# Borders of a two-layer streaming encoder: first rows and weights loaded one stage ahead, input normalisation on three engines

## The reference

```python
x = layernorm(x)                                   # once, ahead of the first layer
for l in range(2):
    h = x @ w_in[l]                                # 1024 -> 7592 columns: q, k, v of three mixers, gates
    oa, ob, oc = forgetting attention, banded attention with sinks, latent attention
    up_n = (o_n * silu(g_n)) @ w_br[l, n]          # n = a, b, c: 512 -> 1024
    mixed = sum_n sigmoid(gate_n) * up_n
    x = layernorm(alpha * x + mixed @ w_o[l])
```

## Time and profile before

| | |
|---|---|
| time, median of 3 runs | 3544.3 us (3537.41, 3544.3, 3546.9) |
| the profiled execution | 3536.73 us, span 3535.1 us |
| TensorE matmul busy | 3212.8 us (91%), 20878 instructions |
| VectorE busy | 1463.6 us (41%) |
| ScalarE busy | 882.9 us (25%) |
| GpSimd busy | 173.4 us (5%) |
| DMA | 421.83 MB, mean 119 GB/s |

### The profile page before, as it was taken

The page is one execution under the profiler, slowest core; times in us unless marked ns, Lnnn a source line. Parts: engine busy times, 40 slices in busy tenths (PEclk is TensorE's granted clock), DMA queues, the critical chain, the costliest instruction groups (busy, mean ns, idle before and its releaser), DMA issues. The chain is left out here.

```text
span 3535.1 us, 52710 instructions
## 1 busy us (share of the span) xinstructions
PE 3212.8 (91%) x20878; PEld 2646.8 (75%) x20878; DVE 1463.6 (41%) x3367; ACT 882.9 (25%) x1990; POOL 173.4 (5%) x118
## 2 busy tenths in 40 slices
PE   0999998999999996989969999989999999977988
PEld 0888897777887774667758888877778887755867
DVE  6214234444454442354631142444445444324556
ACT  1221223333223332220212212223332233322110
POOL 0000000101111100000000000001011111000000
PEclk9999999999999997999979999999999999988999
DMA  5332316423332317664443322362222422096633
GB/s 186 125 106 89 91 48 199 115 69 83 87 104 81 87 34 188 203 237 143 142 143 108 105 92 73 103 198 75 70 78 84 118 80 64 28 279 211 203 128 113
DMA packets 405226, 421.83 MB, mean 119 GB/s; under 512 B 146432, under 2 KB 314240, under 8 KB 402624
## 3 DMA queue, kind: packets, MB, share of 16 engines
q1 hardware_dynamic: 375824, 380.74, 35.0%
q10 hardware_dynamic: 29168, 37.89, 3.3%
HBM read 293.27 MB, written 127.64 MB: 119 GB/s over the span
## 5 line engine op out<-in xcount | busy, mean ns | idle before, releaser
L376 PE MATMUL proj_acc<-proj_wh,keep_xh 128*128 128x512 f32 (+1 forms) x1296 | 503.5, 388 | 12.4 <-DVE proj_wl L340 12.4
L377 PE MATMUL proj_acc<-proj_wl,keep_xh 128*128 128x512 f32 (+1 forms) x1296 | 501.9, 387 | 0.0
L378 PE MATMUL proj_acc<-proj_wh,keep_xl 128*128 128x512 f32 (+1 forms) x1296 | 501.5, 387 | 0.0
L1222 ACT ACTIVATE att_p<-att_ss,att_stat 128x257 f32<-128x257 f32 (+9 forms) x384 | 249.2, 649 | 641.1 <-DVE att_stat L1272 602.3
L1279 DVE COPY att_pt<-att_tr 128x256 f32<-128x256 f32 (+3 forms) x384 | 177.1, 461 | 550.2 <-PE att_tr L1159 549.9
L1272 DVE TENSOR_REDUCE att_stat<-att_ss 128x1 f32<-128x257 f32 (+9 forms) x384 | 245.6, 640 | 117.0 <-PE att_ss L1150 112.5
L1148 PE MATMUL att_ss<-att_kt,att_qt 96*128 96x512 f32 (+7 forms) x768 | 291.2, 487 | 1.4 <-DVE att_kt L1207 1.4
L376 PEld LDWEIGHTS proj_acc<-proj_wh,keep_xh 128*128 128x128 f32 x1296 | 245.3, 189 | 58.7 <-DVE proj_wl L340 13.2
L378 PEld LDWEIGHTS proj_acc<-proj_wh,keep_xl 128*128 128x128 f32 x1296 | 245.0, 189 | 46.2
L377 PEld LDWEIGHTS proj_acc<-proj_wl,keep_xh 128*128 128x128 f32 x1296 | 245.2, 189 | 45.4
L1159 PE MATMUL att_tr<-keep_ident,att_p 128*128 128x128 f32 x1392 | 236.0, 283 | 30.6 <-DVE att_sgt L1295 15.7
(11 more groups left out here) (328 smaller groups left out, 5489.7 us busy)
## 6 DMA issues: line engine op xcount, KB each, us to landing
up_gates<-scratch_gates SPq DMA_DIRECT2D x18, 1536.0 KB, 8.0
scratch_gates<-att_gout SPq DMA_DIRECT2D x208, 128.0 KB, 1.7
proj_raw<-in_w_in SPq DMA_DIRECT2D x48, 512.0 KB, 3.7
att_graw<-in_w_in SPq DMA_DIRECT2D x44, 512.0 KB, 3.9
str_ka<-in_cache_a_kT SPq DMA_DIRECT2D x16, 1024.0 KB, 8.9
str_va<-in_cache_a_v SPq DMA_DIRECT2D x16, 1024.0 KB, 5.4
scratch_sg<-proj_out SPq DMA_DIRECT2D x54, 256.0 KB, 2.1
att_sg<-scratch_sg SPq DMA_DIRECT2D x24, 512.0 KB, 5.7
```

Source lines behind the costliest of these rows:

```text
L376: nc.tensor.matmul(bank, hi, wh[:, u, kt, 0:w], start=kt == 0, stop=False)
L377: nc.tensor.matmul(bank, hi, wl[:, u, kt, 0:w], start=False, stop=False)
L378: mm = nc.tensor.matmul(bank, lo, wh[:, u, kt, 0:w], start=False, stop=kt == KT - 1)
L1222: nc.scalar.activation(p[:, s, place], ss[:, s, place], ACT.Exp, bias=stat[:, m % 4, 0:1], accum_out=stat[:, m % 4, 1:2]).then_inc(exp_rea ...
```

## The change

- Input normalisation is shared by three engines. VectorE does statistics, reciprocal, a new one-column product (minus mean times reciprocal) and the gain; ScalarE scales and shifts (`Identity` with scale and bias); GpSimd adds the bias row. The gain of tile t-1 stands in VectorE's list behind the statistics of tile t. A tile is stored two tiles later, and VectorE waits for gain and bias only behind the first statistics.
- `early2` is kept for the whole program (it also serves as `C["row"]`, which has the same size), and holds three of the four quarters of the next projection's first weights; `C["early"]` holds its first three row tiles. They are loaded at the end of the input normalisation for layer 0 and in the middle (t = 5) of the output stage for layer 1; the load at t = 5 is issued after the second layer too.
- The projection's first tile: two tiles are turned instead of three, tile 0's rows are split, then the weights, then the rows of tiles 1 and 2; TensorE waits for each weight split by itself, and turns tile 2 behind tile 0.
- Up stage: three weight tiles are split before the channels of tile 0; TensorE's first tile waits for each weight split by itself. Of the output stage's weights five tiles are loaded ahead instead of six, and in the sixth place the first mixed rows.
- Output stage: the first mixed rows are in SBUF; three weight tiles are loaded there instead of two.

```diff
+            load_first_weights(sp, C, T, 0, first_loaded)
+            for t in range(EARLIEST):
+                load_first_rows(sp, C, T, t, first_loaded)
+            sp.wait_ge(first_loaded, 16 * (1 + EARLIEST))
...
                 act.wait_ge(var_ready, t + 1)
                 nc.scalar.activation(mv[:, t % 2, 2:3], mv[:, t % 2, 1:2], ACT.Sqrt,
                                      bias=C["eps"][:, 0:1]).then_inc(std_ready, 1)
-                if t >= 1:
-                    store(t - 1)
+                act.wait_ge(scale_ready, t + 1)
+                nc.scalar.activation(x[:, t % N, :], x[:, t % N, :], ACT.Identity, scale=mv[:, t % 2, 3:4],
+                                     bias=mv[:, t % 2, 4:5]).then_inc(centred, 1)
+                if t >= 2:
+                    store(t - 2)
+            store(NT - 2)
...
-            dve.wait_ge(gb_loaded, 32)
+            def by_gain(t):
+                dve.wait_ge(centred, t + 1)
+                nc.vector.tensor_tensor(x[:, t % N, :], x[:, t % N, :], gb[:, 0, :], ALU.mult).then_inc(scaled, 1)
             for t in range(NT):
                 dve.wait_ge(x_loaded[t % N], 16 * (t // N + 1))
-                norm_rows(nc, dve, ch, x[:, t % N, :], gb, st, mv[:, t % 2, :], var_ready, std_ready, t, normed)
+                m = mv[:, t % 2, :]
+                ch.link(nc.vector.bn_stats(st[:, 0, :], x[:, t % N, 0:512]))
+                ch.link(nc.vector.bn_stats(st[:, 1, :], x[:, t % N, 512:1024]))
+                nc.vector.bn_aggr(m[:, 0:2], st[:].rearrange("p a b -> p (a b)")).then_inc(var_ready, 1)
+                if t == 0:
+                    dve.wait_ge(gb_loaded, 32)
+                else:
+                    by_gain(t - 1)
+                dve.wait_ge(std_ready, t + 1)
+                ch.link(nc.vector.reciprocal(m[:, 3:4], m[:, 2:3]))
+                nc.vector.scalar_tensor_tensor(out=m[:, 4:5], in0=m[:, 0:1], scalar=-1.0, in1=m[:, 3:4],
+                                               op0=ALU.mult, op1=ALU.mult).then_inc(scale_ready, 1)
+            by_gain(NT - 1)
+        @block.gpsimd
+        def _(pool):
+            pool.wait_ge(gb_loaded, 32)
+            for t in range(NT):
+                pool.wait_ge(scaled, t + 1)
+                nc.gpsimd.tensor_tensor(x[:, t % N, :], x[:, t % N, :], gb[:, 1, :], ALU.add).then_inc(normed, 1)
...
-    raw = ph.sb("raw", [P, 4, 2, 512])
+    raw_last = ph.sb("raw_last", [P, 2, 512])
+    raw = [C["early2"][:, q, :].rearrange("p (h n) -> p h n", h=2) for q in range(FIRST_Q)] + [raw_last]
...
-            for t in range(NT):
-                if t >= XA:
-                    sp.wait_ge(x_taken, 2 * (t - XA + 1))
+            for t in range(XA, NT):
+                sp.wait_ge(x_taken, 2 * (t - XA + 1))
...
-                pe.wait_ge(x_loaded[t % XA], 16 * (t // XA + 1))
+                if t >= XA:
+                    pe.wait_ge(x_loaded[t % XA], 16 * (t // XA))
...
+                    if by_weights:
+                        pe.wait_ge(w_ready[0], kt + 1)
...
-            for t in range(XA):
+            for t in range(2):
                 turn(t)
-            pe.wait_ge(w_ready[0], KT)
+            pe.wait_ge(xl_made, 2)
             for t in range(NT):
                 pe.wait_ge(xl_made, 2 * (t + 1))
-                tile(0, 0, 512, t)
+                tile(0, 0, 512, t, by_weights=t == 0)
+                if t == 0:
+                    turn(2)
                 if t + XA < NT:
...
-            for q in range(4):
+            for q in range(FIRST_Q, 4):
...
-            for t in range(XA):
-                x_high(t)
+            x_high(0)
             for kt in range(KT):
                 split_hi(act, 0, 0, kt)
+            for t in range(1, XA):
+                x_high(t)
...
-            for t in range(XA):
-                x_low(t)
+            x_low(0)
             for kt in range(KT):
                 split_lo(dve, 0, 0, kt)
+            for t in range(1, XA):
+                x_low(t)
...
-EARLIEST, EARLY = 3, 6
+EARLIEST, EARLY, EARLY_O = 3, 6, 5
...
+FIRST_Q = 3
...
+def load_first_rows(eng, C, T, t, loaded):
+    eng.dma_start(C["early"][:, t, :], T["y_prompt"][0][rows(t)]).then_inc(loaded, 16)
+def load_first_weights(eng, C, T, l, loaded):
+    src = T["w_in"].rearrange("l (kt p) n -> l p kt n", p=P)[l, :, 0:2 * FIRST_Q, ds(CHUNKS[0][1][0][0], 512)]
+    eng.dma_start(C["early2"][:].rearrange("p k (h n) -> p (k h) n", h=2), src).then_inc(loaded, 16)
...
-                    sp.dma_start(C["early2"][:], w_o_tiles(T, l)[:, EARLIEST:EARLY, :]).then_inc(early_loaded, 16)
-            sp.wait_ge(early_loaded, 32)
+                    sp.dma_start(C["early2"][:, 0:EARLY_O - EARLIEST, :], w_o_tiles(T, l)[:, EARLIEST:EARLY_O, :])\
+                        .then_inc(early_loaded, 16)
+                if t == 5:
+                    sp.wait_ge(stored[0], 16)
+                    sp.dma_start(C["early2"][:, EARLY_O - EARLIEST, :], S["mix"][rows(0)]).then_inc(early_loaded, 16)
+            sp.wait_ge(early_loaded, 48)
...
-                        if t == 0 and half == 0:
-                            pe.wait_ge(wl_made, 4 * (n + 1))
                         if t >= 1:
                             pe.wait_ge(up_taken, 6 * (t - 1) + a + 1)
                         cols = slice(512 * half, 512 * half + 512)
                         for k in range(4 * n, 4 * n + 4):
+                            if t == 0 and half == 0:
+                                pe.wait_ge(wl_made, k + 1)
...
-            turned(0)
             for k in range(KB):
+                if k == EARLIEST:
+                    turned(0)
...
-            turned(0, range(3))
             for k in range(KB):
+                if k == EARLIEST:
+                    turned(0, range(3))
...
-        return early_tile(C, k) if k < EARLY else raw[:, k - EARLY, :]
+        return early_tile(C, k) if k < EARLY_O else raw[:, k - EARLY_O, :]
+    def mix_tile(t):
+        return mix[:, t % 2, :] if t else C["early2"][:, EARLY_O - EARLIEST, :]
...
-            load_mix(0)
-            for k in range(EARLY, KT):
+            for k in range(EARLY_O, KT):
...
+                if t == EARLIEST + 2:
+                    sp.wait_ge(wl_made, EARLY_O)
+                    sp.wait_ge(tr_made, 2)
+                    load_first_weights(sp, C, T, DEPTH - 1, first_loaded)
+                    for of in range(EARLIEST):
+                        load_first_rows(sp, C, T, of, first_loaded)
+            sp.wait_ge(first_loaded, 16 * (1 + EARLIEST))
...
-                pe.wait_ge(mix_loaded[u], 16 * (t // 2 + 1))
+                if t:
+                    pe.wait_ge(mix_loaded[u], 16 * ((t + 1) // 2))
...
+        C["early"] = keep("early", [P, EARLIEST, D])
+        C["early2"] = keep("early2", [P, EARLY - EARLIEST, D])
         load_constants(nc, C, T)
         input_norm(nc, C, T)
-        C["early"] = keep("early", [P, EARLIEST, D])
+        C["row"] = C["early2"][:].rearrange("p k n -> p (k n)").rearrange("p (r t c) -> p r t c", r=RING, t=PT)
...
```

More of the change, by code:

```diff
@@ L171, in input_norm @@
     st = ph.sb("st", [P, 2, 6])
-    mv = ph.sb("mv", [P, 2, 4])
-    gb_loaded, chain = ph.sem("gb_loaded"), ph.sem("chain")
+    mv = ph.sb("mv", [P, 2, 5])
+    gb_loaded, chain, first_loaded = ph.sem("gb_loaded"), ph.sem("chain"), ph.sem("first_loaded")
     x_loaded, x_stored = ph.ring("x_loaded", N), ph.ring("x_stored", N)
-    var_ready, std_ready, normed = ph.sem("var_ready"), ph.sem("std_ready"), ph.sem("normed")
+    var_ready, std_ready, scale_ready = ph.sem("var_ready"), ph.sem("std_ready"), ph.sem("scale_ready")
+    centred, scaled, normed = ph.sem("centred"), ph.sem("scaled"), ph.sem("normed")
     xin, xout = T["x_prompt"][0], T["y_prompt"][0]
@@ L289, in load @@
         for col, w in CHUNKS[c][1]:
-            eng.dma_start(raw[:, q, :, at:at + w], w_src[l, :, 2 * q:2 * q + 2, ds(col, w)]).then_inc(raw_loaded[q], 16)
+            eng.dma_start(raw[q][:, :, at:at + w], w_src[l, :, 2 * q:2 * q + 2, ds(col, w)]).then_inc(raw_loaded[q], 16)
             at += w
@@ L324, in _, with raw_loads @@
                 sp.wait_ge(out_stored[j], 16 * (stores_before(NCH - 1, j) + 3 * len(STORES[CHUNKS[-1][0]])))
-        def raw_loads(c):
+        def raw_loads(c, q):
+            came = int(q < FIRST_Q)
             if c >= NCH - 2:
-                return (NCH - 2) + sum(len(parts) for _, parts in CHUNKS[NCH - 2:c + 1])
-            return c + 1
+                return (NCH - 2) + sum(len(parts) for _, parts in CHUNKS[NCH - 2:c + 1]) - came
+            return c + 1 - came
         def split_hi(act, c, u, kt, w=512):
-            act.wait_ge(raw_loaded[kt // 2], 16 * raw_loads(c))
-            nc.scalar.activation(wh[:, u, kt, 0:w], raw[:, kt // 2, kt % 2, 0:w], ACT.Copy).then_inc(wh_made, 1)
+            if raw_loads(c, kt // 2):
+                act.wait_ge(raw_loaded[kt // 2], 16 * raw_loads(c, kt // 2))
```

(33 more changed lines are left out.)

## The result

The changed kernel took 3510.2 us (median of 4 runs, 3506.3 to 3513.4), against 3544.6 us for the kernel before beside it. The ratio is 0.9905, 95% interval 0.9889 to 0.992: faster by about 34 us, and 0.2 us from the forecast. The profiled executions differ by 28.5 us of span, 3535.1 against 3506.6, where the sum of the prediction was 30.0. The closeness is largely luck. The forecast of 3510 was put between the sum on the profiled execution (3506.7) and on the median (3514), the same kernel had medians of 3505.5 and 3501.3 in two later series, and the stages show errors that cancel. (In the experiments, one execution of "both causes out of the normalisation" took 4712.1 us at a granted clock of 0.648 and is left out of its median.)

The account below looks back on a forecast made before the run. TensorE was busy in 91% of the span, with dips at stage borders. Terms 5 - 11.6 - 11.8 - 4.6 - 7.0 = -30.0 gave 3506.7 us on the profiled execution, 3514 on the median; forecast 3510, range 3492 to 3528.

Parts of the forecast that it names:

- Normalisation, +5: Input normalisation: sharing over three engines gains nothing per tile and stores come later, last store at 70.0 against 64.93: +5 us.
- The gate: Normalisation: VectorE's one-column operation, held until GpSimd's addition ends, gates ScalarE's pass; a tile costs 5.5 us.
- The loop: Normalisation: store, load into the reused buffer, statistics, multiply, GpSimd with held operation, and ScalarE take 12.7 us per two tiles.
- Projection 0, -11.6: Layer 0's projection: first matmul at 73.2 instead of 85.86, gain 12.7, less 1.0 for turn(2) moved behind tile 0.
- the stall at the seventh tile: Projection: the 2.08 us stall at 115.20 was expected to move along with the earlier start.
- Projection 1: Layer 1's projection: first matmul 4.6 us behind the start at 1805.0 instead of at 1822.46, less 1.0: -11.8 us.
- Up, -2.3 each: Up stage, each layer: VectorE's queue 3.3 us earlier, TensorE's idle time at tile 1 3.1 us, 1.0 charged for the clock.
- Output, -3.5 each: Output stage, each layer: transposes begin at about 1674.5 instead of 1678.01, extra loads hidden: -3.5 us.
- Rival B: Normalisation: the one-column operation isn't held by GpSimd, so -4 instead of +5, time 3501 us; chance 0.16.
- Rival C: Projections and output stages: starts not bound by loads alone, each loses 3.5 us, total -16, time 3524 us; chance 0.16.
- D: Whole kernel: Rival C plus normalisation at its upper bound and no up-stage gain, about -8, time 3532 us; chance 0.06.
- Rival E: Attention and stream stage: shifted borders lower TensorE's clock, 81 us more at the lower level, time 3560 us; chance 0.04.

Follow-up runs that it names:

- both causes out of the normalisation: Changed kernel with nine row buffers instead of four and the one-column product ahead of the previous tile's multiply in the normalisation: 3480.7 us, ratio 0.9839.
- The edit on tile 1: Changed kernel with VectorE's low parts of the up stage's tile 1 ahead of the mixing of tile 0's second branch: 3489.1 us, ratio 0.9863.

## Why the prediction was right, point by point

- *Normalisation, +5: wrong by 5, measured +0.2 at the projection's start.* The gate was the right one, and even 128x1 is held. The loop was mis-sized, 12.7 against 11.4: I had put ScalarE's pass of 1.1 us ahead of the store, but the queue issues the store 0.01 us after the pass begins (24.71 and 24.72). And the first held product, which I had in the sum, slipped through by 0.04 us, so the first store went at 24.72, not 28.1. Against these, the 3 MB of early loads, which I had as hidden, put 1.1 us between the last store and the projection. The Trainium skill ("SBUF — State Buffer", section "Who interferes with whom") has two-input operations of VectorE contend with a GpSimd that reads SBUF, and issue order decide who waits; the trace agrees in both directions, 2.32 us behind and 0.16 ahead. The same section says that an operation with at most one SBUF input, outside the modes that use both ports, doesn't contend: the statistics beside the addition took 0.69, as alone.
- *Projection 0, -11.6: direction and place right, size -14.2.* The first matmul came where it was put (73.2 predicted, 73.05 measured). Of the missing 2.6 us, 1.7 are the clock's: I assumed that the stall at the seventh tile would cost as before, and it didn't. In the kernel before, the windows at it and behind it were at 0.96 and 0.87:

```profile
105.86:115.86 10.00, 7.92 (x40) 6.45 (x39) 2.19 (x4) 3.13 (x7) 0.00 (x0) 0.96 0.72 231
115.86:125.86 10.00, 10.00 (x46) 8.47 (x46) 5.53 (x10) 5.63 (x11) 0.00 (x0) 0.87 0.80 267
```

  and in the changed kernel, as far behind its first matmul:

```profile
93.05:103.05 10.00, 7.96 (x42) 6.45 (x40) 1.89 (x3) 2.83 (x6) 0.00 (x0) 1.00 0.70 228
103.05:113.05 10.00, 10.00 (x52) 8.30 (x51) 6.35 (x11) 5.93 (x12) 0.00 (x0) 1.00 0.84 270
```

  Projection 1 gained 2.1 more than predicted, by two errors: the first matmul came 5.5 us behind the start, not 4.6, and the clock gave 3.1 back. The granted clock was 0.69 in the ten microseconds from the first matmul before and is 0.83 now, and 0.83 and now 1.00 in the fourth ten. In all other profiles with the new order and early loads each of the two projections is 12 to 17 us shorter than before.
- *Up, -2.3 each: the mechanism right, the clock's price too low.* First matmul 7.6 behind the first DMA (7.5), idle 3.67 (3.1), gains of 3.2 and 0.7. Over all profiles, sixteen up stages in this order take 169.4 to 172.3 us, mean 171.4, and six in the old order 172.1 to 172.9, mean 172.7: the order is worth 1.3 us a layer, and the 1.0 charged for the clock was about 2.0 (3.3 - 1.3). In the ten microseconds from tile 1's first matmul the granted clock was 1.00 in only one of the sixteen (169.4), 0.83 to 0.85 in eight (170.9 to 171.5) and 0.71 to 0.74 in seven (171.7 to 172.3); in the six, behind 0.6 to 1.6 us of idle time, it was always 1.00. The edit on tile 1 shows that the gap was VectorE's queue, as the working had it.
- *Output, -3.5 each: right*, 3.7 and 3.6. The extra DMAs are hidden.
- *Rival B* (not held) fell by the 2.32 us. *Rival C* (starts not bound by loads) fell: the transposes start at once in all four places; D, which rested on it, went with it. What limits the layers' border is still open: 7.2 us lie between the last store and the first instruction (1783.49 to 1790.73), as before, and no run touched it.
- *Rival E* (the clock) was priced by its whole size and so put at 0.04, but a lower clock was at work in small: the stream stages gave back 10.2 us. The two profiles of one kernel show that it needs no edit at all, so these 10.2 us can't be put down to the change. What sets the level in a given execution isn't settled.

## What to carry to other kernels

Before work is shared out to an idle engine, look at what else waits for the two: a 128-element operation queued behind the hand-over cost 2.2 us a tile and, with the buffer loop, took all that the sharing won; moved in front of it, and with the loop opened too, the sharing gave 15 us. Two limits of like size have to go together, since each alone gave 0.3 to 0.4 of it. Loads that are issued early must also have landed before the last store of the stage, or they delay its end (1.1 us here, by comparing traces). And a stage's length should be compared with a second profile of the same kernel before a difference is given a cause: here an untouched stage moved by 7 us and the first pair of profiles gave the up stage of layer 0 a gain of 3.2, where the mean over all is 1.3.

## What the runs showed of the hardware

- A 128x1 operation with two SBUF inputs on VectorE lasts as long as GpSimd's running 128x1024 addition (2.32 us for 0.16), and an order of 0.03 to 0.04 us decides it.
- ScalarE's queue issues a DMA while the pass ahead of it is running (0.01 us behind its start).
- With 3 MB of loads in flight (DMA share 1.04, 424 GB/s) the next stage began 4.8 us behind the last store, against 3.7 without.
- A stall of 3.67 us of TensorE, taken away, gave 2.8 us against the stage in which the granted clock had stayed up behind it, and 5.3 and 6.3 against those in which it had fallen (0.76 in the ten microseconds at 3243.47); the same stall did the one in layer 0 and the other in layer 1 of one execution. At the same place the clock fell within ten microseconds behind 15 of 16 stalls of 2.3 to 3.7 us, and behind none of six of 0.6 to 1.6 us.
- The stream stage, with the same 1030 matmuls, took 144.6 to 157.2 us at granted clocks of 0.90 to 0.82.
